# MoE decoder layer: a norm half moved to GpSimd, one expert in 2 MB loads, a list spread over a stage

## The chip, the cores and the metric

The kernel runs on one core of one Trainium2 chip. The metric is the device time of one execution in microseconds (us), the median of several. TensorE (PE) multiplies, VectorE (DVE), ScalarE (ACT) and GpSimd (POOL) work on tiles of 128 partitions, and SyncE (SP) issues the loads from HBM.

## What is computed

A decoder trunk of one layer for 256 tokens of 1024 features in float32: a Mamba-2 mixer, cross-attention into a memory of 256 rows, and a mixture of 32 experts of which each token takes four; then a final norm. Almost all bytes are expert weights: per expert gate_up is 1024 x 2048 and down 1024 x 1024 in float32, 12.58 MB together, 402.7 MB for 32.

```python
    h = h + moe_ffn(rms_norm(h, ffn_norm[i]), w_router, b_router, w_gate_up, b_gate_up, w_down, b_down)
    return rms_norm(h, final_norm)

    # moe_ffn
    logits = (ht @ w_router).astype(jnp.float32) + b_router.astype(jnp.float32)
    top_logits, top_idx = lax.top_k(logits, TOP_K)
    gates = jax.nn.softmax(top_logits, axis=-1)
    ...
        gu = xb @ w_gate_up[e] + b_gate_up[e]
        gate = jnp.minimum(gu[..., :D_FF], SWIGLU_LIMIT)
        up = jnp.clip(gu[..., D_FF:], -SWIGLU_LIMIT, SWIGLU_LIMIT)
        act = (up + 1.0) * (gate * jax.nn.sigmoid(gate * SWIGLU_ALPHA))
        return act @ w_down[e] + b_down[e]
```

## The kernel before

The program is written per engine: each engine has its own list of instructions, ordered by hand, and semaphores tie them together. Mixer and attention take about the first 320 us. What follows is the token norm and the routing, and then the experts.

**Norm and routing.** VectorE adds the attention's output to `h` in four parts (L1800, semaphore `h_ok`). ScalarE squares `h` and takes the root of the mean (semaphore `std`). VectorE then makes `xn`, the normed tokens times the gains `g_ffn`, for tokens 0 to 127 (`norm_chunk(3, 0, ...)`, L1488). The gains are applied in an order in which source and gain are read at a stride of four elements. It computes the router's logits, the largest eight (L1818), the mask of the chosen experts (L1826), then `xn` for tokens 128 to 255 (`norm_apply(3, 1, ...)`, L1488 again, semaphore `normed`). TensorE counts meanwhile from the mask which place each token has with its expert (L933 to L935), between filler matmuls (L914). VectorE makes rank (L1831) and the one-hot matrix of the first two experts (L1834, semaphore `hot_ok`). TensorE's first gather (L946) waits for `hot_ok` and for `normed`. SP waits for `normed` too, before it loads the last two rows of expert 1's gate_up over `h` and `g_ffn`.

**Experts.** Each expert has 64 slots for each of up to four chunks of its tokens; the first 64 tokens are handled in the regular stage, and what overflows would be worked off after the experts from a list (with these inputs TensorE also has to know whether there is one). A stage `regular(i, c)` is expert `2i + c`. On TensorE it is: transposes of the scatter rows (L968), gate_up as 64 matmul instructions in four quarters (L985, semaphore `gu_used` after each), for odd experts half of the gather for the next pair (L960), the down product of the expert before in two halves (L1013, semaphore `dn_used`), transposes of this expert's gate_up for VectorE (L1000), the scatter of the expert before into four banks of sums (L1023), and for odd experts the other half of the gather. VectorE reads out gate_up (L1863), adds biases (L1871) and does SwiGLU up to L1882. Even and odd experts' gate_up weights have a buffer each (`ring`, `odd_ring`, 8 MB), and down has one of 4 MB (`ring`).

**Loads.** SP issues the weights in order. Expert 3 and 31 come in four pieces of 2 MB, each when `gu_used` says that this quarter of the buffer is read (`reload_pieces`, L376); other experts in two groups of 4 MB, each when two quarters are read (`reload_gate_up`, L390). Down comes in two halves of 2 MB (L379). From expert 5 on SP runs a loop over pairs.

**Middle.** Between experts 16 and 17 TensorE leaves its loop and runs `biases_and_list`: it transposes the gates (L1081), which ScalarE copies into `scatT`, multiplies them with the down biases into the sums (L1087), counts tokens (L1091), and goes forward and back with VectorE to make the list of overflowing chunks (L1094 to L1098). All engines then read the number of its entries.

## Time and profile before

| | us |
|---|---|
| median of 3 runs | 1248.57 |
| the runs | 1247.25, 1248.57, 1249.79 |
| the profiled execution | 1247.7 |
| its span in the trace | 1245.9 |
| TensorE busy | 1175.0 (94%) |
| VectorE busy | 391.1 (31%) |
| ScalarE busy | 275.9 (22%) |
| GpSimd busy | 7.5 (1%) |
| DMA, mean over the span | 365 GB/s, 454.30 MB |

The span is what the trace covers; the execution's own time is 1.8 us longer. All times in rows are counted from the span's start. Mean rates tell little here, since the first third loads little. A row of windows gives for a stretch: its length, busy time and instruction count of PE, of its weight loads (PEld), of DVE, ACT and POOL, then TensorE's granted clock as a share of 2.4 GHz, the mean busy share of the 16 DMA engines, and GB/s. A row of the chain gives start, length and what the end of the program was waiting for at that time. A row of a timeline gives start, length, engine, line, operation, output and input with shapes, and in brackets how long the engine had been idle and who ended that. An SP row's time is that of the issue, and its length covers several issues where it says x2. A row of groups gives line, engine, operation, shapes and count, then busy time in us and the mean of one in ns.

### The profile page before, as it was taken

The page shows a single profiled execution, that of the slowest core. Times are in us where ns is not written, and L with a number is a line of the kernel's source. Part 1 is how long each engine was busy: PE and PEld are TensorE (multiplying, and loading weights), DVE is VectorE, ACT ScalarE, POOL GpSimd, SP SyncE. Part 2 cuts the span into 40 slices and gives each one's busy share as a digit, 9 for nine tenths or more (in the row PEclk, how much of TensorE's full clock was granted, in tenths as well). Part 3 has the DMA queues.
Part 4 walks back from the last instruction along what each step waited for, and adds up shares of the span by engine and source line. Part 5 has one row for each costly group of instructions (what it writes and reads, how often), then busy time and mean ns, then how long its engine had stood idle before and what let it go on. Part 6 is the DMA issues. An engine that isn't in the chain of part 4 may idle for free.

```text
span 1245.9 us, 15217 instructions
## 1 busy us (share of the span) xinstructions
PE 1175.0 (94%) x6198; PEld 621.5 (50%) x6198; DVE 391.1 (31%) x703; ACT 275.9 (22%) x421; POOL 7.5 (1%) x27
## 2 busy tenths in 40 slices
PE   9999999999999999998988999899999998999996
PEld 8998887898634433333333333334433333343432
DVE  5987677546312211111111112102211111112112
ACT  5655566345211101011000011001101011011102
POOL 1000000000000000000000000000000000000000
PEclk9999999999999999999999999989999999999999
DMA  9454333469799999999999999999999999999996
GB/s 340 155 203 142 129 135 136 162 262 378 304 407 413 434 426 429 431 431 430 433 433 430 429 436 426 433 417 430 436 426 430 429 431 430 432 423 428 432 424 249
DMA packets 49191, 454.30 MB, mean 365 GB/s; under 512 B 5692, under 2 KB 5860, under 8 KB 30084
## 3 DMA queue, kind: packets, MB, share of 16 engines
q1 hardware_dynamic: 48976, 453.73, 87.7%
q8 instruction: 26, 0.43, 0.1%
q10 hardware_dynamic: 180, 0.07, 0.0%
q14 instruction: 9, 0.07, 0.0%
HBM read 452.74 MB, written 1.05 MB: 364 GB/s over the span
## 4 chain that ended last, share of the span: by engine, by line
PE 53%; DMA 42%; DVE 3%; issue 1%; DVEq 1%; SPq 1%; ACT 0%
DMA ring<-in_moe_w_down 41%; PE ps L985 14%; PE ps L1013 11%; PE ps L647 3%; PE ps L649 3%; PE ps L648 3%; PE ps L1023 2%; PE ps L960 2%; PE ps L662 1%; PE ps L664 1%; PE ps L663 1%; PE ps L779 1%; DMA wring<-in_ssd_w_in 1%; DVE wlo L1504 1%; PE ps L1000 1%
## 5 line engine op out<-in xcount | busy, mean ns | idle before, releaser
L1013 PE MATMUL ps<-ring,wring 128*64 128x512 f32 x960 | 216.5, 597 | 49.3 <-DMA ring<-in_moe_w_down 49.3
L985 PE MATMUL ps<-odd_ring,wring 128*64 128x512 f32 x1024 | 225.5, 598 | 0.9 <-DVE wring L1871 0.8
L985 PE MATMUL ps<-ring,wring 128*64 128x512 f32 x1024 | 223.5, 594 | 0.0
L1136 ACT ACTIVATE wring<-ps 128x512 f32<-128x512 f32 (+2 forms) x101 | 52.4, 535 | 499.8 <-PE ps L985 424.4
L1013 PEld LDWEIGHTS ps<-ring,wring 128*64 128x64 f32 x960 | 65.1, 137 | 188.7 <-issue 112.5
L1863 DVE COPY wring<-ps 128x512 f32<-128x512 f32 x32 | 22.1, 691 | 404.7 <-PE ps L985 404.7
L985 PEld LDWEIGHTS ps<-odd_ring,wring 128*64 128x64 f32 x1024 | 73.7, 138 | 141.6 <-issue 139.6
L985 PEld LDWEIGHTS ps<-ring,wring 128*64 128x64 f32 x1024 | 71.9, 137 | 139.3 <-issue 139.1
L1871 DVE TENSOR_TENSOR wring<-ps,bguT 128x512 f32<-128x512 f32 x64 | 41.2, 685 | 296.7 <-PE ps L1000 296.7
L1136 ACT ACTIVATE ysb<-ps 128x512 f32<-128x512 f32 x36 | 21.4, 596 | 260.6 <-PE ps L1013 246.4
L960 PEld LDWEIGHTS ps<-wring 128*128 128x128 f32 x480 | 55.8, 191 | 23.5 <-issue 23.5
L1023 PE MATMUL ps<-ysb,wring 64*128 64x512 f32 x256 | 63.6, 615 | 0.7 <-ACT ysb L1136 0.7
L960 PE MATMUL ps<-wring 128*128 128x128 f32 x480 | 61.5, 281 | 0.0
L1504 DVE TENSOR_TENSOR wlo<-wring,lo_ring 128x2048 fp32r<-128x2048 f32 x23 | 52.2, 2286 | 11.3 <-ACT lo_ring L1136 11.3
L1136 ACT ACTIVATE lo_ring<-wring 128x2048 fp32r<-128x2048 f32 x24 | 45.4, 1930 | 10.1 <-PE ps L649 5.6
L664 PE MATMUL ps<-hi_ring,wlo 128*128 128x256 f32 x160 | 45.3, 283 | 0.0
L1000 PEld LDWEIGHTS ps<-cst,wring 128*128 128x128 f32 x256 | 27.4, 141 | 26.9 <-issue 25.2
L648 PE MATMUL ps<-wlo,hi_ring 128*128 128x512 f32 x96 | 37.4, 389 | 0.0
L1000 PE MATMUL ps<-cst,wring 128*128 128x128 f32 x256 | 35.0, 280 | 0.9 <-DVE wring L1863 0.9
L1136 ACT ACTIVATE wring<-wring 128x512 f32<-128x512 f32 x32 | 20.2, 630 | 60.7 <-DVE wring L1875 60.7
L1023 PEld LDWEIGHTS ps<-ysb,wring 64*128 64x128 f32 x256 | 22.0, 186 | 22.5 <-issue 20.9
L1538 DVE SCALAR_TENSOR_TENSOR ring<-ps,parT,ring 128x255 f32<-128x255 f32 (+2 forms) x72 | 31.1, 476 | 1.8
(312 smaller groups left out, 1311.6 us busy)
## 6 DMA issues: line engine op xcount, KB each, us to landing
ring<-in_moe_w_down SPq DMA_DIRECT2D x59, 2048.0 KB, 25.3
ring<-in_moe_w_gate_up SPq DMA_DIRECT2D x28, 4096.0 KB, 22.9
odd_ring<-in_moe_w_gate_up SPq DMA_DIRECT2D x26, 4096.0 KB, 24.7
wring<-in_ssd_w_in SPq DMA_DIRECT2D x9, 2048.0 KB, 8.5
odd_ring<-in_moe_w_gate_up SPq DMA_DIRECT2D x9, 2048.0 KB, 15.7
ring<-in_moe_w_down SPq DMA_DIRECT2D x10, 1024.0 KB, 33.8
wring<-in_xa_w_kv SPq DMA_DIRECT2D x4, 2048.0 KB, 8.0
wring<-in_ssd_w_out SPq DMA_DIRECT2D x4, 2048.0 KB, 7.9
```

The source lines that it names most:

```text
L647: mm(ps[bank][:, :], xh[:, k0 + k, tok], wh, start=start and k == 0, stop=False)
L648: mm(ps[bank][:, :], xh[:, k0 + k, tok], wl, start=False, stop=False)
L649: last = mm(ps[bank][:, :], xl[:, k0 + k, tok], wh, start=False, stop=stop and k == KD - 1)
L664: last = mm(dst, wl[:, c0:c0 + P], x_hl[0][:, k, :], start=False, stop=k == KD - 1)
L960: last = mm(ps[G_BANK][:, P * m:P * (m + 1)], xn[:, t, P * k:P * (k + 1)], onehot[:, t, :, :], start=t == 0, stop=t == TC - 1)
L985: last = mm(ps[a][SLOTS * half:SLOTS * (half + 1), :], xs[:, m, c % 2, :], w[:, kk, c0:c0 + 512], start=s + kk == 0, stop=s + kk == GP)
L1000: last = tr(ps[a][:, P * j:P * (j + 1)], gus[:, c0:c0 + P], ident)
L1013: last = mm(ps[D_BANK][SLOTS * half:SLOTS * (half + 1), :], act[:, k, :], w[:, kk, 512 * half:512 * (half + 1)], start=k == 0, stop=k == K ...
L1023: last = mm(ps[4 + 2 * t + half][:, :], rows[r, P * t:P * (t + 1)], ysb[r, :], start=False, stop=True, skip_group_check=True)
L1136: return nc.scalar.activation(out_, in_, func, **kw)
L1504: v.tensor_tensor(lo_, raw_, hi.bitcast(F32), ALU.subtract).then_inc(wl_ok, 1)
L1871: v.tensor_tensor(gu[:, a, :, :, :], ps[a][:, :].rearrange("p (j h s) -> p j h s", j=4, h=2), b4[:, a, :, :].unsqueeze(3).to_broadcast([P, ...
```

## The change

- GpSimd gets two instructions behind its last one: the product of `h` and `g_ffn` for tokens 128 to 255, once `std` says that the root is done, and the product with the reciprocal root, once VectorE has made that (new semaphore `rst_ok`). The second raises `normed`. VectorE's L1488 for these tokens goes.
- Expert 4's gate_up comes in four pieces of 2 MB like expert 3's.
- SP's loop goes; its issues are written out per expert, in the same order. The counts of the semaphores `g_ready` are computed by a new `transfers`.
- TensorE's pairs 0 and 1 are written out, the loop runs over pairs 2 to 7, pair 8 is written out, and a second loop runs over 9 to 14.
- `biases_and_list` is split into four parts, which run inside the stage of expert 18 instead of between 16 and 17. The gates' transposes go to another PSUM bank (3 instead of 2) and are copied by ScalarE to a place of their own, `gateT`. VectorE's part is split in two, ahead of SwiGLU and behind it.

VectorE's rows at the norm, before (L1824 takes the chosen logits out, L1826 makes the mask, L1831 rank, L1834 the one-hot):

```order
L1824 MATCH_REPLACE rank<-mx,lg 128x32 x2
L1826 TENSOR_TENSOR mask<-rank,lg 128x64
L1488 SCALAR_TENSOR_TENSOR wring<-hs,rst 128x1024
L1831 SCALAR_TENSOR_TENSOR rank<-ps,mask 128x2x32
L1834 TENSOR_TENSOR wring<-iota,rank 128x256
```

And now (lines are 36 to 38 higher in the changed kernel):

```order
L1862 MATCH_REPLACE rank<-mx,lg 128x32 x2
L1864 TENSOR_TENSOR mask<-rank,lg 128x64
L1867 SCALAR_TENSOR_TENSOR rank<-ps,mask 128x2x32
L1870 TENSOR_TENSOR wring<-iota,rank 128x256
L1875 TENSOR_TENSOR gate<-gate,mask 128x64
```

The norm of the second token half left VectorE's list. It stands at the end of GpSimd's, behind the products of the mixer (`lo_ring`) that were GpSimd's last work:

```order
L561 CAST iota<-iota_i 128x128
L562 CAST col<-col_i 128x3
L566 TENSOR_TENSOR lo_ring<-by,rank 128x1024 x2
L571 TENSOR_TENSOR wring<-hs 128x1024
L576 TENSOR_SCALAR wring<-wring,rst 128x1024
```

The last two rows are new. SP's rows from expert 3's pieces on, before (`odd_ring` 128x4096 is a 2 MB piece, 128x8192 a 4 MB group):

```order
L376 DMA odd_ring<-in_moe_w_gate_up 128x4096 x4
L379 DMA ring<-in_moe_w_down 128x4096 x2
L390 DMA ring<-in_moe_w_gate_up 128x8192 x2
L379 DMA ring<-in_moe_w_down 128x4096 x2
L492 UNCONDITIONAL_BRANCH
```

And now:

```order
L381 DMA odd_ring<-in_moe_w_gate_up 128x4096 x4
L384 DMA ring<-in_moe_w_down 128x4096 x2
L381 DMA ring<-in_moe_w_gate_up 128x4096 x4
L384 DMA ring<-in_moe_w_down 128x4096 x2
L395 DMA odd_ring<-in_moe_w_gate_up 128x8192 x2
```

The third row, expert 4, is four pieces now, and no loop follows. TensorE's rows at the list, before, from the end of expert 16's stage (L1013 down, L1000 transposes, L1023 scatter) to expert 17's gate_up:

```order
L1013 MATMUL ps<-ring,wring 64x512 x16
...
L1000 MATMUL ps<-cst,wring 128x128 x8
L1023 MATMUL ps<-ysb,wring 128x512 x4
...
L1081 MATMUL ps<-cst,gate 32x128 x2
L1087 MATMUL ps<-wring 128x512 x4
L1091 MATMUL ps<-cst,mask 128x1 x2
L1094 MATMUL ps<-cnt,cst 128x1
L1096 MATMUL ps<-pick,col 1x16
...
L968 MATMUL ps<-cst,wring 128x128 x2
...
L985 MATMUL ps<-odd_ring,wring 64x512 x32
```

And now, inside expert 18's stage (L999 gate_up, L1027 down, L1014 transposes, L1037 scatter):

```order
L1082 MATMUL ps<-cst,gate 32x128 x2
L999 MATMUL ps<-ring,wring 64x512 x32
L1091 MATMUL ps<-wring,wdt 128x512 x4
L1095 MATMUL ps<-cst,mask 128x1 x2
L1027 MATMUL ps<-ring,wring 64x512 x16
L1101 MATMUL ps<-cnt,cst 128x1
L1014 MATMUL ps<-cst,wring 128x128 x8
L1037 MATMUL ps<-ysb,wring 128x512 x4
L1106 MATMUL ps<-pick,col 1x16
L1107 MATMUL ps<-pick,col 1x16
L1108 MATMUL ps<-cst,cnt 1x1
L1148 TENSOR_LOAD lst_i
```

The same products stand between the stage's own parts; the reading of the count (L1148) still follows the last of them. The diff, cut to its core:

```diff
@@ -59,6 +59,9 @@
 GS = GR // 2
 RSLOTS = 8
 MIDDLE = 8
+
+BY_PIECES = (3, 4, 31)
+AHEAD = ((0, 4), (25, 2), (26, 0))
 HSLOTS = 4
 WARM = 17
 
...
+        gateT = part(wdt_f, 0, SEQ)
...
-        def g_loads(n, c):
-
-
-            extra = (0 if n == GP + 1 else 1) if n >= GP else 0 if c < 2 else 1 if n else 2
-            if n % GS == 0:
-                return c // 2 + 1 + extra
-            return min(c // 2, 1) + 1 + extra + (1 if n >= GP and c >= NE - 1 else 0)
+        def transfers(n, e):
+
+
+            if e % 2 != n // GP:
+                return 0
+            if e == 1:
+                return 1 if n == GP + 1 else 2
+            if e == 2:
+                return 2 if n else 3
+            return 1 if e == 0 or e in BY_PIECES or n % GS == 0 else 0
+
+        def g_loads(n, e):
+            return sum(transfers(n, x) for x in range(e + 1))
...
-            def reload_pieces(e):
-
-                for s in range(GP):
+            def reload_pieces(e, pieces_):
+
+                for s in pieces_:
                     sp.wait_ge(gu_used, GP * (e - 2) + s + 1)
                     load_gate_up(sp, e, e % 2, s)
...
-            reload_pieces(3)
-            reload_down(1, 0, 1)
-            reload_gate_up(4, 0, 4)
-            reload_down(2, 0, 2)
-            with sp.Fori(1, PAIRS - 4, 1) as i:
-                for c in (1, 2):
-                    reload_gate_up(2 * i + (c + 2), i, c + 2)
-                    reload_down(2 * i + c, i, c)
-            reload_gate_up(NE - 5, 0, NE - 5, range(0, GJ // 2))
-            reload_down(NE - 7, 0, NE - 7)
-            reload_gate_up(NE - 5, 0, NE - 5, range(GJ // 2, GJ))
-            for e in range(NE - 6, NE - 3):
-                reload_down(e, 0, e)
-                reload_gate_up(e + 2, 0, e + 2)
-            reload_down(NE - 3, 0, NE - 3)
-            reload_pieces(NE - 1)
+            for c in range(1, NE - 2):
+                e = c + 2
+                ahead = [n for first, n in AHEAD if c >= first][-1]
+                for part_, s0, s1 in ((0, 0, ahead), (1, ahead, GP)):
+                    if part_:
+                        reload_down(c, 0, c)
+                    if e in BY_PIECES:
+                        reload_pieces(e, range(s0, s1))
+                    else:
+                        reload_gate_up(e, 0, e, range(s0 // GS, s1 // GS))
...
+            pool.wait_ge(ld_g, 16)
+            pool.wait_ge(std, 2 * 3 + TC)
+            nc.gpsimd.tensor_tensor(xn[:, 1, :].rearrange("q (k p) -> q k p", k=GR),
+                                    h[:, 1, :].rearrange("q (p k) -> q k p", k=GR),
+                                    g_ffn.rearrange("q (p k) -> q k p", k=GR), ALU.mult)
+            pool.drain()
+            pool.wait_ge(rst_ok, 1)
+            nc.gpsimd.tensor_scalar(xn[:, 1, :], xn[:, 1, :], rst[:, 3, 1:2], None, ALU.mult).then_inc(normed, 1)
...
-                    pe.wait_ge(g_ready[n], 16 * i + 16 * g_loads(n, c) if n % GS == 0 else 16 * g_loads(n, expert))
+                    pe.wait_ge(g_ready[n], 16 * i + 16 * (g_loads(n, expert) - (expert - c) // 2) if n % GS == 0 else
+                               16 * g_loads(n, expert))
...
-            def regular(i, c, expert, gathers=True):
-
-                scatter_transpose(i, c)
-                pe.wait_ge(gate_b, 2 * i + c)
-                pe.wait_ge(up_b, 2 * i + c)
-                gate_up(i, c, expert)
-                if gathers:
-                    gather_half(i, 1, 0)
-                down(i, c - 1)
-                transposes(i, c)
-                scatter(i, c - 1)
-                if gathers:
-                    gather_half(i, 1, 1)
-
-            def biases_and_list():
+            def turn_gate():
 
                 pe.wait_ge(gate_ok, 1)
+                pe.wait_ge(xsb_ok, MIDDLE + 2)
                 for t in range(TC):
-                    last = tr(ps[D_BANK][0:NE, P * t:P * (t + 1)], gate[:, t, :], ident)
+                    last = tr(ps[G_BANK][0:NE, P * t:P * (t + 1)], gate[:, t, :], ident)
                 last.then_inc(gT_ps, 1)
+
+            def biases_and_counts():
+
                 pe.wait_ge(gT_ok, 1)
                 pe.wait_ge(ld_bdn, 16)
                 for n in range(2):
                     for t in range(TC):
-                        mm(ps[4 + 2 * t + n][:, :], scatT[0:NE, P * t:P * (t + 1)],
+                        mm(ps[4 + 2 * t + n][:, :], gateT[0:NE, P * t:P * (t + 1)],
                            bdn[0:NE, 512 * n:512 * (n + 1)], start=False, stop=True, skip_group_check=True)
                 pe.wait_ge(mask4_ok, 1)
                 for t in range(TC):
-                    last = mm(ps[D_BANK][:, 256:257], mask4[:, t, :], ones[:, 0:1], start=t == 0, stop=t == TC - 1)
+                    last = mm(ps[G_BANK][:, 256:257], mask4[:, t, :], ones[:, 0:1], start=t == 0, stop=t == TC - 1)
                 last.then_inc(cnt_ps, 1)
+
+            def places():
+
                 pe.wait_ge(val_ok, 1)
-                mm(ps[D_BANK][:, 258:259], stri, cnt[:, 0:1], start=True, stop=True).then_inc(pos_ps, 1)
+                mm(ps[G_BANK][:, 258:259], stri, cnt[:, 0:1], start=True, stop=True).then_inc(pos_ps, 1)
+
+            def overflow_list():
+
                 pe.wait_ge(pick_ok, 1)
-                mm(ps[D_BANK][0:1, 272:288], col[:, 0:1], pick[:, :], start=True, stop=True)
-                mm(ps[D_BANK][0:1, 288:304], col[:, 1:2], pick[:, :], start=True, stop=True)
-                mm(ps[D_BANK][0:1, 304:305], cnt[:, 0:1], ones[:, 0:1], start=True, stop=True).then_inc(lst_ps, 1)
-                pe.wait_ge(lst_ok, 1)
+                mm(ps[G_BANK][0:1, 272:288], col[:, 0:1], pick[:, :], start=True, stop=True)
+                mm(ps[G_BANK][0:1, 288:304], col[:, 1:2], pick[:, :], start=True, stop=True)
+                mm(ps[G_BANK][0:1, 304:305], cnt[:, 0:1], ones[:, 0:1], start=True, stop=True).then_inc(lst_ps, 1)
+
+            def regular(i, c, expert, gathers=True, lists=False):
+
+                scatter_transpose(i, c)
+                if lists:
+                    turn_gate()
+                pe.wait_ge(gate_b, 2 * i + c)
+                pe.wait_ge(up_b, 2 * i + c)
+                gate_up(i, c, expert)
+                if lists:
+                    biases_and_counts()
+                if gathers:
+                    gather_half(i, 1, 0)
+                down(i, c - 1)
+                if lists:
+                    places()
+                transposes(i, c)
+                scatter(i, c - 1)
+                if lists:
+                    overflow_list()
+                if gathers:
+                    gather_half(i, 1, 1)
 
             pe.wait_ge(hot_ok, 1)
...
-            regular(0, 1, 1)
-            regular(0, 2, 2, False)
-            with pe.Fori(1, MIDDLE, 1) as i:
-                regular(i, 1, 3)
-                regular(i, 2, 4, False)
-            biases_and_list()
+
+            for i in range(0, 2):
+                regular(i, 1, 2 * i + 1)
+                regular(i, 2, 2 * i + 2, False)
+            with pe.Fori(2, MIDDLE, 1) as i:
+                regular(i, 1, 5)
+                regular(i, 2, 6, False)
+            regular(MIDDLE, 1, 2 * MIDDLE + 1)
+            regular(MIDDLE, 2, 2 * MIDDLE + 2, False, True)
+            pe.wait_ge(lst_ok, 1)
             extra = pe.value_load(lst_i[0:1, 32:33], min_val=0, max_val=MAX_EXTRA)
-            with pe.Fori(MIDDLE, PAIRS - 1, 1) as i:
-                regular(i, 1, 3)
-                regular(i, 2, 4, False)
+            with pe.Fori(MIDDLE + 1, 15, 1) as i:
+                regular(i, 1, 2 * MIDDLE + 3)
+                regular(i, 2, 2 * MIDDLE + 4, False)
             last_experts(PAIRS - 1)
...
-            def regular(i, c, gathers=True):
+            def regular(i, c, gathers=True, lists=False):
 
                 scatter_out(i, c)
+                if lists:
+                    act_.wait_ge(gT_ps, 1)
+                    fn(gateT[0:NE, :], ps[3][0:NE, 0:SEQ], ACT.Copy).then_inc(gT_ok, 1)
...
-            act_.wait_ge(gT_ps, 1)
-            fn(scatT[0:NE, :], ps[2][0:NE, 0:SEQ], ACT.Copy).then_inc(gT_ok, 1)
+            regular(MIDDLE, 1)
+            regular(MIDDLE, 2, False, True)
             act_.wait_ge(lst_ok, 1)
             extra = act_.value_load(lst_i[0:1, 32:33], min_val=0, max_val=MAX_EXTRA)
-            with act_.Fori(MIDDLE, PAIRS - 1, 1) as i:
+            with act_.Fori(MIDDLE + 1, PAIRS - 1, 1) as i:
...
-            v.reciprocal(rst[:, 3, 1:2], nrm[:, 3, 1:2])
+            v.reciprocal(rst[:, 3, 1:2], nrm[:, 3, 1:2]).then_inc(rst_ok, 1)
...
-            norm_apply(3, 1, xn, h, g_ffn)
-            dve.drain()
...
-            def regular(i, c, gathers=True, out=act):
+            def regular(i, c, gathers=True, out=act, lists=False):
...
+                if lists:
+                    overflow_places()
                 swiglu(i, c, 2 * i + c, out)
-
-            def overflow_list():
+                if lists:
+                    overflow_list()
+
+            def overflow_places():
...
+            def overflow_list():
+
...
-            overflow_list()
+            regular(MIDDLE, 1)
+            regular(MIDDLE, 2, False, lists=True)
```

## Rows read from the trace of the kernel before

**Rows 1.** Windows: stretch, length, engines' busy times, clock, DMA share, GB/s.

```profile
324.00:348.00 24.00, 22.42 (x112) 12.47 (x114) 7.09 (x27) 3.37 (x6) 0.00 (x0) 0.93 0.84 315
384.00:400.00 16.00, 16.00 (x78) 5.38 (x76) 0.69 (x1) 0.60 (x1) 0.00 (x0) 1.00 0.97 400
460.00:800.00 340.00, 307.21 (x1514) 118.81 (x1510) 55.50 (x120) 31.40 (x57) 0.00 (x0) 1.00 1.00 431
800.00:835.00 35.00, 31.14 (x134) 12.58 (x135) 6.44 (x19) 2.58 (x5) 0.00 (x0) 0.85 1.00 421
```

**Rows 2.** The chain that ended last: start, us, what.

```profile
817.49 15.92 PE ps L985 x64
...
1073.11 13.88 PE ps L985 x64
...
1093.86 1.02 PE ps L1000 x8
...
1097.16 13.88 PE ps L985 x64
...
1125.19 13.88 PE ps L985 x64
```

**Rows 3.** SP's timeline: issues of weight loads.

```profile
328.90 0.80 SPq L383 DMA_DIRECT2D odd_ring<-in_moe_w_gate_up  x2
335.39 1.19 SPq L460 DMA_DIRECT2D ring<-in_moe_w_gate_up  x2
...
387.56 7.19 SPq L390 DMA_DIRECT2D ring<-in_moe_w_gate_up  x2
...
826.77 7.16 SPq L390 DMA_DIRECT2D odd_ring<-in_moe_w_gate_up  x2
```

**Rows 4.** The chain at the middle, between experts 16 and 17.

```profile
804.54 1.03 PE ps L1000 x8
...
808.27 4.21 PE ps L1087 x8
812.48 0.96 PE ps L1091 x4
...
815.72 1.09 issue
```

**Rows 5.** VectorE's timeline at the norm, and the end of expert 16's SwiGLU.

```profile
322.74 2.13 DVE L1488 SCALAR_TENSOR_TENSOR wring<-hs,rst 128x1024 f32<-128x1024 f32 x1
...
326.69 0.22 DVE L1826 TENSOR_TENSOR mask<-rank,lg 128x64 f32<-128x64 f32 x1
326.83 2.05 DVE L1488 SCALAR_TENSOR_TENSOR wring<-hs,rst 128x1024 f32<-128x1024 f32 x1
...
329.28 0.43 DVE L1834 TENSOR_TENSOR wring<-iota,rank 128x256 f32<-128x256 f32 x1
...
808.28 0.69 DVE L1882 TENSOR_TENSOR wring<-wring 128x512 f32<-128x512 f32 x1
```

**Rows 6.** TensorE's timeline from the rank counts to the first gather.

```profile
327.43 0.39 PE L935 MATMUL ps<-mask,cst 128*128 128x32 f32 x2
...
329.80 4.43 PE L946 MATMUL ps<-wring 128*128 128x128 f32 x23 [1.04 <-DVE wring L1834]
```

**Rows 7.** Groups by line: busy us, mean ns of one.

```profile
L1504 DVE TENSOR_TENSOR wlo<-wring,lo_ring 128x2048 fp32r<-128x2048 f32 x23 | 52.2, 2286 | 11.3 <-ACT lo_ring L1136 11.3
L1488 DVE SCALAR_TENSOR_TENSOR wring<-hs,rst 128x1024 f32<-128x1024 f32 x2 | 4.2, 2090 | 0.1
L561 POOL TENSOR_TENSOR lo_ring<-by,rank 128x1024 fp32r<-128x1024 f32 x2 | 3.8, 1898 | 116.8 <-PE ps L649 116.8
L1485 DVE TENSOR_SCALAR ring<-hs,rst 128x1024 f32<-128x1024 f32 x2 | 1.5, 754 | 0.2
```

**Rows 8.** ScalarE's timeline: the root for tokens 128 to 255.

```profile
322.74 0.29 ACT L1136 ACTIVATE nrm<-nrm 128x1 f32<-128x1 f32 x1
```

**Rows 9.** Timeline of GpSimd and VectorE in the mixer.

```profile
122.28 3.75 POOL L561 TENSOR_TENSOR lo_ring<-by,rank 128x1024 fp32r<-128x1024 f32 x2 [116.81 <-PE ps L649]
...
125.00 3.18 DVE L1504 TENSOR_TENSOR wlo<-wring,uth 128x2048 fp32r<-128x2048 f32 x1
```

11 lines of the change are left out of this document (6 added, 5 removed).

## The prediction

> **What bounds the kernel now.** I read the bandwidth of stretches first, then the chain, then SP's timeline, and the busy shares last: TensorE is busy 94% and the DMA engines are full as well, so shares decide nothing. From 460 to 800 us the stream runs at 431 GB/s with a DMA share of 1.00 [rows 1]; that is its ceiling in this trace. One expert's weights are 12.58 MB, at 431 GB/s 29.2 us. TensorE alone needs less: where it waits for nothing, gate_up groups of the same parity start at 1073.11 and 1125.19 [rows 2], so two experts take 52.08 us and one 26.04. It has 3.2 us to spare per expert.
>
> So from about 340 to 1230 us the kernel is a stream of bytes. **A microsecond counts only if it lets the stream run earlier or closes a stretch below 431.** Such a stretch loses its length times (1 - rate/431): 324 to 348 us loses 6.5, 384 to 400 loses 1.15, 800 to 835 loses 0.81 [rows 1]. The change touches all three. That the chain names PE from 1068 on does not contradict this: TensorE sets the times of the issues there, and the queue is still filled.
>
> **Expert 4 in 2 MB pieces.** SP issues its first group at 387.56 [rows 3], because 4 MB wait for two quarters of expert 2's gate_up. The stream runs down meanwhile; that is the 1.15 us. A gate_up takes 13.88 [rows 2], a quarter of it 3.47, so the first 2 MB can be issued at 384.1, 3.5 us earlier, three times the sag. The second piece is issued at 387.56 as before and needed 4.9 us (2.1 MB at 431 GB/s) behind the first. Later groups are issued as before; TensorE frees 12.58 MB in 26.0 us, which the stream needs 29.2 for, so the margin only grows. **Gain 1.15 us**, bounds 0 (something else than the late issue makes the sag) and 1.3 (its edges too). The two more issues on SP cost nothing: SP waits for TensorE between them.
>
> **List and biases inside expert 18's stage.** In a plain stage gate_up starts 3.30 us behind the transposes (1093.86 to 1097.16 [rows 2]). At the middle the transposes start at 804.54, and gate_up not at 807.84 but at 817.49: bias products 4.21, counts 0.96, rounds with VectorE up to 815.72, and 1.09 of reading the count [rows 2, 4]. That is 9.7 us; and this gate_up takes 15.92 instead of 13.88 [rows 2], in a stretch whose mean granted clock is 0.85 [rows 1]. Sum 11.7 us. The issue that hangs on it came at 826.77 [rows 3], so some 11.7 late, and the stream lost only 0.81. So 10.9 us of delay are free here and only what exceeds them costs.
> Now, in expert 18's stage: 0.8 to turn the gates (transposes and copy, up to 808.27 from the 807.5 at which scatter is done), 4.2 and 1.0, together 6.0 us ahead of the down product, of which 3.2 are spare: 2.8 late. Behind it: the places product, 0.6, a quarter of the 2.3 us between 813.44 and 815.72 [rows 4]; then VectorE ends SwiGLU 4.4 us behind the transposes' start (804.54 to 808.97 [rows 4, 5]), the list takes 0.5 more, reading it 1.09, the scatter rows' transposes 0.3: 6.3 against 3.3 in a plain stage, 3.0 late. Sum 6.4; with 2.0 for a fall of the clock 8.4, below 10.9. TensorE catches up 3.2 per expert, by expert 21. What is queued behind its wait for the list is expert 19's gate_up, and for that waits SP's group for expert 21; both are in the 8.4. VectorE waits for the counts ahead of SwiGLU, whose transposes come behind the down product anyway. **Gain 0.8 us**, bounds 0 and 0.85; over 11.7 it would turn into a loss, 1 us for 1 us.
>
> **The queue written out, loops cut differently.** SP's loop and register steps go, TensorE leaves out a turn of its loop: covered by the waits of both in these stages. Zero, bounds -0.2 and 0.2, estimates from the 3.2 of spare time that would have to fail first.
>
> **The token norm's second half on GpSimd.** This is the uncertain term, because it moves the start of the experts, on which everything up to 384 us hangs. Before, L1488 for tokens 128 to 255 runs on VectorE for 2.05 us from 326.83, behind mask (326.69), and rank and one-hot follow until 329.71; the first gather starts 329.80, 1.04 behind the last filler matmul [rows 5, 6]. Without L1488 the rank counts decide: TensorE ends them at 327.82 (327.43 + 0.39 [rows 6]), then rank 0.3 and one-hot 0.5 make 328.6, or 328.4 with no pauses. A gain of 1.2 to 1.4 us, if GpSimd is done by then.
> GpSimd does it in two steps: a product of h and g_ffn, 128x1024, both read at a stride of four elements, and the product with the scalar. Its only product in this trace, 128x1024 with plain or repeated operands, took 1.90 us [rows 7]. What the stride does shows on VectorE: L1504 takes 2.29 for 2048 contiguous elements, so 1.14 for 1024, and L1488 takes 2.09 for 1024 [rows 7], a factor of 1.8. So the product takes between 1.9 and 3.4; I take the middle, 2.65. The scalar step lies between 0.75 (VectorE's L1485) and 1.9 (GpSimd's product); I take the middle, 1.3 [rows 7]. The root it needs is ready at 323.03 [rows 8].
> It may not start there. GpSimd's second product ended at 126.03; L1504 on VectorE, begun 125.00, took 3.18 instead of 2.29 [rows 7, 9]. So an instruction of VectorE with two operands in SBUF and a GpSimd product did not run at once; the later one waited. Now L1488 for tokens 0 to 127 holds VectorE from 322.74 for 2.13 us [rows 5], so the product runs 324.9 to 327.55. Mask has two SBUF operands, is due 326.69 and waits until 327.55; the rank counts end 328.65. The scalar step runs 327.65 to 328.95, rank beside it (one operand in PSUM), the one-hot, two SBUF operands, 329.0 to 329.5. First gather at 329.6 instead of 329.8: **gain 0.2 us**. Bounds: a gain of 1.4 (nothing collides), and with 3.4 and 1.9 for the two steps the one-hot ends 330.75, a loss of 1.1. I take the value between, since the collision has a row and its absence has none.
> The Trainium skill, SBUF — State Buffer, section "Who interferes with whom", calls this an exclusive lock on a port pair that the two engines share, and the trace agrees for L1504 (3.18 against 2.29). The Trainium skill, GPSIMD Engine Reference, section "Performance pitfalls for Q7 kernels", has reads at a stride over 8 bytes cost half again as much: an estimate of 2.85 us for the product by it, with which the forecast would be 0.2 us later; no run here shows it yet.
> SP too waits for this norm before the last two rows of expert 1, issued 328.90 [rows 3]. Those 2 MB take 4.9 us, and the next issue at 335.39 [rows 3] waits for TensorE; what they win by being earlier is lost there unless TensorE is earlier. So only the first gather's time counts.
>
> **Sum.** 1.15 + 0.8 + 0 + 0.2 = 2.1 us. The profiled execution took 1247.7 us (span 1245.9): 1245.6. The median of three is 1248.57, 0.87 above it; carried over, 1248.57 - 2.1 = **1246.5 us**, 0.17% less, under the 0.2% (2.5 us) that a measurement of this kernel can tell from no change.
>
> **Rivals.**
> (a) GpSimd is hidden whole, first gather at 328.4. For it: its wait is met at 323.03, 5.4 us ahead. Against: L1504's 3.18. Total 1.15 + 0.8 + 1.4 = 3.35, 1245.2; if the pause of 1.04 goes and with it the fall of the clock (mean 0.93 over 24 us [rows 1], that is 3.4 us at half clock, 1.7 lost), 1243.5.
> (b) The collision is worse: the small one-source instruction ahead of mask (L1820) waits for the product as well. Then match_replace and mask are due only at about 328.3, the scalar step is running, and mask starts 329.0; rank counts 1.1, rank and one-hot 0.8, gather 330.9, 1.1 late. Total 1.15 + 0.8 - 1.1 = 0.85: 1247.7. No row shows such an instruction beside GpSimd. The Trainium skill, SBUF — State Buffer, section "Who interferes with whom", says that a tensor_scalar in a 2-port mode takes the pair as well.
> (c) The sags move instead of closing: with SP's issues tied to TensorE, what the stream gains is lost at a later issue point. Total 0.2: 1248.4. Against: TensorE is faster than the stream everywhere behind.
> (d) Slower: GpSimd's product on strided operands is far dearer. Each microsecond over 2.65 delays the first gather by one; at 4.75 all gains are spent, and from 7.25, nearly four times the row's 1.90, the loss can be told. At 8 us: 1246.5 + 5.35 = 1251.8. Against: the factor of 1.8 on VectorE.
>
> **Chances.** Forecast 0.35, (a) 0.25, (b) 0.20, (c) 0.12, (d) 0.08. Under 1246.07 it is faster by over 0.2%: nearly all of (a), and 0.15 of the rest, as the forecast lies 0.4 us from that line while three runs spread over 2.5: 0.40. Slower: (d) and 0.01 of spread, 0.09. Within: 0.51. Range: low 1243.8 (the clock case less some of its 1.7), high 1249.3 ((c) and 0.9 of spread); (d) is left out.
>
> **What would show it.** Windows of the changed kernel: 384 to 400 at 430 GB/s, else the pieces did nothing; around experts 19 to 21 at 430, else the list came too late, and SP's issue for expert 21 says by how much. GpSimd's two rows give their start and length; a product that starts beside L1488 and takes under 3 us refutes the collision, a mask that starts late confirms it, late steps ahead of it confirm (b). The first gather, against the last addition to h, gives the norm term. If both sags are closed and the stream ends less than 1 us earlier though the gather is not late, the view of the kernel as a stream is wrong.

## The result, and the profile after

The changed kernel took **1250.38 us** (median of 20 runs, 1249.44 to 1251.22). The kernel before, run beside it, took 1246.43 (20 runs, 1244.95 to 1249.79); the ratio is **1.0031, interval 1.0024 to 1.0037**, 3.95 us slower. The forecast was 0.17% faster, with a chance of 0.09 for "slower by over 0.2%". It was wrong in sign. The profiled execution took 1249.45 (span 1247.7), 1.75 more than the one before, which with 1247.7 was one of the later ones of its kernel. The 20 times of the kernel before fall mostly into two groups, near 1245.5 and near 1247.4; what may part them comes below.

Windows after (length, engines' busy times, granted clock, DMA share, GB/s), and behind them the window of before at 1090 us:

```profile
324.00:348.00 24.00, 20.23 (x104) 11.72 (x105) 8.22 (x26) 3.27 (x6) 7.51 (x2) 0.93 0.74 274
384.00:400.00 16.00, 16.00 (x76) 5.32 (x74) 0.69 (x1) 0.60 (x1) 0.00 (x0) 1.00 1.00 427
800.00:835.00 35.00, 31.02 (x152) 11.81 (x150) 5.29 (x13) 2.81 (x5) 0.00 (x0) 1.00 1.01 431
1090.00:1100.00 10.00, 10.00 (x52) 3.86 (x50) 2.88 (x7) 1.63 (x4) 0.00 (x0) 1.00 0.85 333
```

```profile
1090.00:1100.00 10.00, 10.00 (x50) 3.81 (x48) 4.60 (x12) 1.61 (x3) 0.00 (x0) 1.00 0.97 390
```

Against [rows 1]: both slow stretches did close, 400 to 427 GB/s and 421 to 431. The start got worse (315 to 274), and a stretch at 1090 us, which the prediction does not mention, fell from 390 to 333.

The start, on GpSimd, VectorE and TensorE of the changed kernel (timelines: start, us, operation):

```profile
323.08 5.58 POOL L571 TENSOR_TENSOR wring<-hs 128x1024 f32<-128x1024 f32 x1 [197.11 <-ACT nrm L1171]
328.84 2.85 POOL L576 TENSOR_SCALAR wring<-wring,rst 128x1024 f32<-128x1024 f32 x1 [0.18 <-issue]
```

```profile
322.64 2.12 DVE L1526 SCALAR_TENSOR_TENSOR wring<-hs,rst 128x1024 f32<-128x1024 f32 x1
...
325.82 2.86 DVE L1858 TENSOR_SCALAR gsum<-mx 128x2 f32<-128x2 f32 x1
...
329.27 0.76 DVE L1864 TENSOR_TENSOR mask<-rank,lg 128x64 f32<-128x64 f32 x1
...
331.27 0.42 DVE L1870 TENSOR_TENSOR wring<-iota,rank 128x256 f32<-128x256 f32 x1
```

```profile
330.08 0.41 PE L946 MATMUL ps<-mask,cst 128*128 128x32 f32 x2 [3.77 <-DVE mask L1864]
...
331.84 4.48 PE L959 MATMUL ps<-wring 128*128 128x128 f32 x24
336.25 4.08 PE L999 MATMUL ps<-ring,wring 128*64 128x512 f32 x18
```

GpSimd's product holds VectorE's L1858, an instruction of two elements per partition that takes 0.17 us otherwise (the same instruction at 325.93 in before), for 2.86 us, until the product ends. Mask, 326.69 before [rows 5], starts at 329.27. The first gather starts at 331.84 instead of 329.80 [rows 6], gate_up at 336.25 instead of 334.27. The Trainium skill, SBUF — State Buffer, section "Who interferes with whom", has a tensor_scalar wait too; the 2.86 agrees. Beside GpSimd's second instruction the wait was short: mask, with two operands in SBUF, began inside it (328.84 to 331.69) and took 0.76 us instead of 0.22, and the one-hot at 331.27 took its usual 0.42. The norm (331.69) and the one-hot (331.69) end together, so either alone would have held the gather as long. SP's issue that waits for the norm comes at 331.72 instead of 328.90.

The issues on SP (timeline):

```profile
337.37 1.19 SPq L471 DMA_DIRECT2D ring<-in_moe_w_gate_up  x2
...
386.10 10.63 SPq L381 DMA_DIRECT2D ring<-in_moe_w_gate_up  x4
...
880.36 7.20 SPq L395 DMA_DIRECT2D odd_ring<-in_moe_w_gate_up  x2
```

Expert 4's first 2 MB go out at 386.10, 1.46 ahead of the group before [rows 3] although everything is 2 us late: 3.4 us were won, as forecast. The middle of the changed kernel, TensorE in expert 18's stage:

```profile
855.60 3.69 PE L1091 MATMUL ps<-wring,wdt 32*128 32x512 f32 x8
859.22 0.60 PE L1095 MATMUL ps<-cst,mask 128*128 128x1 f32 x4
859.76 7.09 PE L1027 MATMUL ps<-ring,wring 128*64 128x512 f32 x32
...
867.02 1.07 PE L1014 MATMUL ps<-cst,wring 128*128 128x128 f32 x8
...
872.87 0.43 PE L981 MATMUL ps<-cst,wring 128*128 128x128 f32 x2 [2.64 <-issue]
873.23 3.23 PE L999 MATMUL ps<-odd_ring,wring 128*64 128x512 f32 x14
```

Gate_up starts 6.2 us behind the transposes of the stage before (867.02 to 873.23) instead of 3.3, so 2.9 late (forecast 3.0); no sag follows.

### The profile page after: what moved, and what is told of

Same layout as the page of the kernel before. It is cut to its first block, busy times and chain, and to the rows that moved or that the text cites. A ratio compares the mean times of both kernels' runs of the same rounds, so it can differ in the third digit from the quotient of the medians.

```text
span 1247.7 us, 14882 instructions
## 1 busy us (share of the span) xinstructions
PE 1173.3 (94%) x6198; PEld 621.4 (50%) x6198; DVE 392.5 (31%) x702; ACT 276.3 (22%) x421; POOL 15.9 (1%) x29
## 3 DMA queue, kind: packets, MB, share of 16 engines
HBM read 452.74 MB, written 1.05 MB: 364 GB/s over the span
## 4 chain that ended last, share of the span: by engine, by line
PE 56%; DMA 41%; DVE 1%; issue 1%; SPq 0%; ACT 0%; DVEq 0%; POOL 0%; POOLq 0%
DMA ring<-in_moe_w_down 41%; PE ps L999 13%; PE ps L1027 11%; PE ps L660 3%; PE ps L662 3%; PE ps L661 3%; PE ps L675 2%; PE ps L676 2%; PE ps L677 2%; PE ps L973 2%; PE ps L1037 2%; PE ps L647 1%; PE ps L792 1%; PE ps L1014 1%; PE ps L771 1%; PE ps L770 1%
## 5 line engine op out<-in xcount | busy, mean ns | idle before, releaser
L1027 PE MATMUL ps<-ring,wring 128*64 128x512 f32 x960 | 218.0, 600 | 51.2 <-DMA ring<-in_moe_w_down 51.2
L999 PE MATMUL ps<-odd_ring,wring 128*64 128x512 f32 x1024 | 223.3, 594 | 0.8 <-DVE wring L1907 0.8
L999 PE MATMUL ps<-ring,wring 128*64 128x512 f32 x1024 | 223.5, 594 | 0.0
L1027 PEld LDWEIGHTS ps<-ring,wring 128*64 128x64 f32 x960 | 65.5, 137 | 191.3 <-issue 114.2
L1171 ACT ACTIVATE wring<-ps 128x512 f32<-128x512 f32 (+1 forms) x100 | 52.1, 537 | 490.7 <-PE ps L999 422.3
L999 PEld LDWEIGHTS ps<-odd_ring,wring 128*64 128x64 f32 x1024 | 73.2, 137 | 139.5 <-issue 137.8
L999 PEld LDWEIGHTS ps<-ring,wring 128*64 128x64 f32 x1024 | 72.0, 137 | 139.3 <-issue 139.1
L1037 PE MATMUL ps<-ysb,wring 64*128 64x512 f32 x256 | 63.6, 615 | 0.7 <-ACT ysb L1171 0.7
L1014 PEld LDWEIGHTS ps<-cst,wring 128*128 128x128 f32 x256 | 27.5, 141 | 26.1 <-issue 24.3
L1014 PE MATMUL ps<-cst,wring 128*128 128x128 f32 x256 | 34.9, 279 | 0.9 <-DVE wring L1899 0.9
L1037 PEld LDWEIGHTS ps<-ysb,wring 64*128 64x128 f32 x256 | 22.0, 186 | 22.5 <-issue 20.9
```

Of the source, the lines that this page charges most:

```text
L999: last = mm(ps[a][SLOTS * half:SLOTS * (half + 1), :], xs[:, m, c % 2, :], w[:, kk, c0:c0 + 512], start=s + kk == 0, stop=s + kk == GP)
L1014: last = tr(ps[a][:, P * j:P * (j + 1)], gus[:, c0:c0 + P], ident)
L1027: last = mm(ps[D_BANK][SLOTS * half:SLOTS * (half + 1), :], act[:, k, :], w[:, kk, 512 * half:512 * (half + 1)], start=k == 0, stop=k == K ...
L1037: last = mm(ps[4 + 2 * t + half][:, :], rows[r, P * t:P * (t + 1)], ysb[r, :], start=False, stop=True, skip_group_check=True)
L1171: return nc.scalar.activation(out_, in_, func, **kw)
```

## The experiments

All ratios stand against the kernel before, run on the same chip, with 95% intervals. The expectations name three theories, A, B and C; C is that the norm's move is the whole loss and the rest of the change is worth nothing in the end.

### Taking the change apart

```diff
 # norm_back: the changed kernel, norm on VectorE again
-            pool.wait_ge(ld_g, 16)  ... (both GpSimd instructions)
+            norm_apply(3, 1, xn, h, g_ffn)
 # norm_only: the kernel before, with that block on GpSimd and nothing else
 # no_pieces: norm_back, with
-BY_PIECES = (3, 4, 31)
+BY_PIECES = (3, 31)
 # queue_only: the kernel before, with SP's queue written out as in the change, expert 4 in groups
 # list_only: the kernel before, with only list and biases inside expert 18's stage (pair 8 written out for it)
```

> The changed kernel with the norm of tokens 128 to 255 back on VectorE; expert 4's pieces, the list in expert 18's stage and the written-out queue stay. Theory A (the pace of the stream is set by the slowest of the 16 DMA engines; the sags at 384 and 826 us were only the faster engines waiting for it, and what else the change costs comes with the written-out code): first gather back at 329.8, and about 1.8 us slower than before (ratio 1.0014). Theory B (the stream's mean rate counts, each closed sag gives its loss): about 2 us faster than before (0.9984). Rival C (the norm costs all of the 3.9): same as before.

> The kernel before with nothing but the norm of tokens 128 to 255 moved to GpSimd. All theories: GpSimd's product again about 5.6 us, the small tensor_scalar of VectorE near 2.9 us, the first gather 2.1 us later. Theories A and B: 2.1 us slower than before (1.0017). Rival C: 3.9 us slower (1.0031).

> As e1_norm_back, and expert 4 in 4 MB groups again; list in the stage and written-out queue stay. Theory A: the same as e1_norm_back within 0.3 us; the sag at 384 to 400 is back in the mean rate, but the slowest DMA engine ends expert 4's groups no later. Theory B: 1.1 us slower than e1_norm_back.

> The kernel before with only SP's queue written out per expert, same order and sizes. Theory A: between 0 and 1 us slower, since the additional instruction fetches go through the DMA engines and each holds one of them for about 0.6 us. Theory B: 0, and a tie would also say that the remaining cost lies with TensorE's written-out pairs or the list.

> The kernel before with only the overflow list and biases inside expert 18's stage. Theory C (a stretch in which the stream runs under 431 GB/s is the faster DMA engines waiting for the slowest, and closing it gives nothing): the stretch 814 to 843 us runs at 430 GB/s instead of 418, and the ratio is 1.0000, within 0.0006. Rival (bytes count one for one): 0.8 us faster, 0.9993.

> The changed kernel itself, beside the others on the same chip. Its ratio should be 1.0031 again; it is what the two kernels with more or fewer steps are compared with. If the parts add, it equals the norm's part (1.0036) plus what the rest is worth (1.0005 by the kernel without the norm's part, 0.9998 by the queue alone), that is 1.0030 to 1.0041.

```
kernel                    median   ratio   interval
norm on VectorE again     1245.70  1.0005  0.9996 to 1.0014
norm's move alone         1248.95  1.0036  1.0022 to 1.0050
norm again, no pieces     1246.38  1.0006  0.9997 to 1.0016
SP's queue alone          1245.92  0.9998  0.9989 to 1.0007
list and biases alone     1245.50  0.9997  0.9988 to 1.0006
the changed kernel again  1250.10  1.0031  1.0021 to 1.0041
```

The norm's move carries the whole loss. Everything else together is 1.0005: a gain of 1.95 us (0.9984, theory B) is outside its interval, a loss of 1.0014 (A) at its edge. The norm's move alone excludes the 1.0017 of A and B. C is the one that holds. In that run's profile the first gather came at 332.94, 3.1 us late instead of the expected 2.1, but it ran faster, and gate_up started at 336.27 as in the changed kernel. With the list alone the stretch did close:

```profile
814.00:843.00 29.00, 25.71 (x136) 11.40 (x134) 4.73 (x9) 3.67 (x7) 0.00 (x0) 1.00 1.01 432
```

It ran at 418 GB/s before, and 432 brought 0.4 us with an interval of -0.7 to +1.5; the 0.8 of the forecast is not excluded by this run alone, and the pieces alone (1.0005 against 1.0006) are not told apart either. Only their sum is.

That comparison says little about a closed sag, for there was none to close. From 384 to 400 us, first without the pieces and then in pool_cost (the kernel before, but for three idle-time instructions on GpSimd, see below):

```profile
384.00:400.00 16.00, 16.00 (x79) 5.46 (x76) 0.69 (x1) 1.05 (x2) 0.00 (x0) 1.00 1.03 427
384.00:400.00 16.00, 16.00 (x78) 5.49 (x75) 0.69 (x1) 0.96 (x2) 0.00 (x0) 1.00 1.02 423
```

The expectation that the sag would be back was wrong. It is deepest in before (400) and in SP's queue alone (406), the two profiles of VectorE's norm in its old place in which TensorE's clock fell at the gather, so that gate_up started at 334.2. There the 4 MB group was issued at 387.5, here, with gate_up at 332.5 and 332.6, at 385.8 and 385.9.

### What the move on GpSimd costs

```diff
 # pool_cost: the kernel before, three extra instructions on GpSimd while VectorE is idle
+            pool.wait_ge(gu_part, 1)
+            nc.gpsimd.tensor_tensor(bdn..."q (k p) -> q k p", xn[:, 1, :]..., xn[:, 0, :]..., ALU.mult)
+            pool.drain()
+            nc.gpsimd.tensor_scalar(bdn, bdn, rst[:, 3, 1:2], None, ALU.mult)
+            pool.drain()
+            nc.gpsimd.tensor_tensor(bdn, xn[:, 1, :], xn[:, 0, :], ALU.mult)
```

> The kernel before with three more instructions on GpSimd while VectorE has nothing with two operands in SBUF to do (behind the first group of gate_up): a product of 128x1024 with the strides that the changed kernel's has, a product with a scalar, and a product of 128x1024 with plain operands; their result is overwritten by the down biases. If the 5.58 us of the changed kernel's product hold a wait for VectorE's L1526 (until 324.76, 1.7 us), the strided one takes 3.8 to 3.9 here; if they hold none, 5.6. Scalar step: 1.9 to 2.1 if the mask's 0.5 was in the 2.85, else 2.85. Plain product: 1.9 as in the trace of before.

```profile
333.78 4.04 POOL L567 TENSOR_TENSOR wring<-wring 128x1024 f32<-128x1024 f32 x1 [207.78 <-PE ps L995]
338.00 2.85 POOL L571 TENSOR_SCALAR wring<-wring,rst 128x1024 f32<-128x1024 f32 x1 [0.18 <-issue]
341.00 2.36 POOL L573 TENSOR_TENSOR wring<-wring 128x1024 f32<-128x1024 f32 x1
```

With nothing beside it the strided product takes 4.04 us, the plain one 2.36 (expected 1.9), the scalar step 2.85. So the 5.58 hold 1.5 to 1.7 of waiting for L1526 (which ends at 324.76), and the scalar step's 2.85 holds no wait. The stride costs a factor of 1.7. The Trainium skill, GPSIMD Engine Reference, section "Performance pitfalls for Q7 kernels", has half again as much; measured against the plain product here it is 1.7.

### Is it GpSimd, or only the late gate_up?

```diff
 # norm_first: the kernel before, nothing on GpSimd, VectorE's norm (and half of it twice) ahead of mask
+            norm_half(0)
+            dve.drain()
+            norm_apply(3, 1, xn, h, g_ffn)
             v.tensor_tensor(mask[:, :, :], rest, lg[:, :, :], ALU.not_equal).then_inc(mask_ok, 1)
-            norm_apply(3, 1, xn, h, g_ffn)
 # fillers, fillers_8: the changed kernel, TensorE kept busy in the wait for mask
-            keep_warm(1, 3)
+            keep_warm(1, 16)     (fillers)
+            keep_warm(1, 8)      (fillers_8)
```

> The kernel before with nothing on GpSimd, but with VectorE's scaling of tokens 128 to 255 (2.05 us) ahead of the mask instead of behind it, and ahead of that a scaling of half its columns (1.13 us) which is done again by it and serves only to take time. The mask is then ready at about 330.0 and the first gather at 331.8, as in the changed kernel, with the same 3.8 us in which TensorE is idle. Theory C (only the time at which gate_up can begin counts, whoever causes it): gate_up starts at 336.2, ratio 1.0031 (1.0022 to 1.0036). Rival G (GpSimd's instructions do harm beyond the late mask, by their traffic or at the end of the norm): at most 1.0020.

> The changed kernel, with 13 more filler matmuls on TensorE in the 3.8 us in which it waits for the mask ahead of the rank counts. GpSimd and VectorE do what they do in the changed kernel, so the first gather stays at 331.8. Theory K (a part of the loss is TensorE's clock, which falls to half behind this longer gap): the granted clock does not fall at 331 us, the first gathers take 2.9 us for 24 instead of 4.5, gate_up starts at 334.7 instead of 336.25, and the kernel is 1.3 to 1.6 us faster than the changed kernel on the same chip, ratio 1.0020 against the kernel before. Theory L (the lateness of the gather alone): no difference to the changed kernel, ratio 1.0031. Rival: the fall only comes later, as it does in other profiles (505, 854 us), with the same result as L.

> The changed kernel with 5 more filler matmuls in the 3.8 us in which TensorE waits for the mask, where the run with 13 more had made TensorE itself 1.5 us late (gather at 333.4, yet gate_up at 336.23 as the gathers ran at full clock). Some 2.1 us are filled and 1.7 stay open, more than the 1.04 behind which the clock falls in some executions of the kernel before. Theory K (time = gate_up's start; clock falls behind an idle stretch of TensorE, but not always behind a short one): where it does not fall, gather at 331.85, gate_up at 334.7, span 1.5 us shorter than the changed kernel's, ratio 1.0019; where it falls as before, 336.25 and 1.0031. So a ratio between 1.0019 and 1.0031, and in the profiled execution gate_up's start and the granted clock at 331 say which. Theory L (lateness of the gather alone): 1.0031 in either case.

Measured: norm_first 1250.90, ratio 1.0040 (1.0026 to 1.0054); fillers 1249.31, 1.0020 (1.0010 to 1.0030); fillers_8 1249.10, 1.0025 (1.0016 to 1.0034). TensorE's timeline in norm_first, then in fillers, then in fillers_8:

```profile
330.00 0.64 PE L933 MATMUL ps<-mask,cst 128*128 128x32 f32 x2 [3.68 <-DVE mask L1838]
...
333.15 4.27 PE L946 MATMUL ps<-wring 128*128 128x128 f32 x24
337.35 3.23 PE L985 MATMUL ps<-ring,wring 128*64 128x512 f32 x14
```

```profile
333.38 2.92 PE L959 MATMUL ps<-wring 128*128 128x128 f32 x24
336.23 4.08 PE L999 MATMUL ps<-ring,wring 128*64 128x512 f32 x18
```

```profile
330.15 0.41 PE L946 MATMUL ps<-mask,cst 128*128 128x32 f32 x2 [1.62 <-DVE mask L1864]
...
331.95 4.35 PE L959 MATMUL ps<-wring 128*128 128x128 f32 x24
336.23 4.08 PE L999 MATMUL ps<-ring,wring 128*64 128x512 f32 x18
```

Norm_first loses as much as the changed kernel without touching GpSimd, so a late mask is enough for the loss and rival G's limit of 1.0020 is excluded. It is not the same wait to the end: the clock fell at 329.3, inside TensorE's idle time, so that the gather started at 333.15 and gate_up at 337.35, 1.1 later than expected. A harm of GpSimd's own of up to about 1 us would not show beside that. Norm_first also parts the two things that are late in the changed kernel: here SP's issue behind the norm came at 329.84, 1.9 earlier than there, and it did not help; gate_up did count. In fillers the gather starts 1.5 us later still, since the fillers themselves run until 331.8, but it runs at 2.4 GHz throughout (2.92 us for 24 instead of 4.48) and gate_up starts at the same 336.23. The expectation that the gather would stay at 331.8 was a miscount of the fillers. In fillers_8 the clock fell in spite of the 5 more fillers, and gate_up starts at 336.23 again. So theory K's best case, gate_up at 334.7, was not met by either, and whether these two win anything against the changed kernel (1.0020 and 1.0025 against 1.0031) is open: the intervals overlap. Theory L is wrong in that gate_up, not the gather, marks the time: fillers has the latest gather of all and is not slower.

### An earlier gather

```diff
 # norm_split: the kernel before, norm in two halves of 128x512
             v.tensor_tensor(mask[:, :, :], rest, lg[:, :, :], ALU.not_equal).then_inc(mask_ok, 1)
-            norm_apply(3, 1, xn, h, g_ffn)
+            norm_half(0).then_inc(half_ok, 1)
...          (behind the one-hot)
+            norm_half(1).then_inc(normed, 1)
 # TensorE: wait for half_ok ahead of first_gather(0, ...), for normed ahead of first_gather(1, ...)
 # split_all: the same in the changed kernel (early pieces, list in stage 18, queue written out)
```

> The kernel before, with VectorE's scaling of tokens 128 to 255 cut into two instructions of 128x512 (the columns of the gathers' first half, then of the second); the second stands behind the one-hot, and TensorE waits for it ahead of the second group of gathers. Nothing goes to GpSimd. Theory C (what the changed kernel lost is the lateness of the first gather, 1 us for 1 us or a little more): the half instruction takes 1.0 to 1.1 us and ends before the rank counts (327.8), the one-hot ends about 1.0 earlier, the first gather starts at about 328.8 instead of 329.8, and the kernel is 0.9 to 1.0 us faster, ratio 0.9992. Rival (a start of the experts that is earlier is lost again at the later sags, as the early pieces were): the gather is 1.0 earlier and the ratio is 1.0000. Rival (the clock): with a gap of only 0.1 us ahead of the gather TensorE's clock does not fall at 330 us, and the gain is 1.0 + 1.4 = 2.4 us, ratio 0.998.

> The changed kernel with the norm on VectorE again, in two halves of 128x512 as above: early pieces, list inside expert 18's stage, queue written out, and the earlier first gather. Theory C: first gather at 328.8 and what the halves give alone, 0.9 to 1.0 us, beside 0 for the rest: ratio 0.9992 (0.9985 to 1.0000). Rival (the closed sags let an earlier start through, which the open ones would swallow): faster than the halves alone by 0.5 to 1.0 us, ratio 0.9985. Rival (skew of the DMA engines takes all of it): 1.0005 as without the halves.

> The changed kernel with the norm split on VectorE, once more: ratio 0.9989 again, 0.9980 to 0.9998, if the gain is real; 1.0000 if it was chance. By gate_up's start (331.7 against 332.7 to 334.3) it should be 1.0 us faster or more.

Norm_split: 1245.04, ratio 0.9992 (0.9982 to 1.0001). Split_all: 1245.03, 0.9989 (0.9979 to 0.9998), and when run again 1245.39, 0.9994 (0.9985 to 1.0003). VectorE and TensorE in norm_split:

```profile
326.79 1.13 DVE L1488 SCALAR_TENSOR_TENSOR wring<-hs,rst 128x512 f32<-128x512 f32 x1
328.01 0.23 DVE L1842 SCALAR_TENSOR_TENSOR rank<-ps,mask 128x64 f32<-128x64 f32 x1
328.31 0.43 DVE L1845 TENSOR_TENSOR wring<-iota,rank 128x256 f32<-128x256 f32 x1
328.65 1.14 DVE L1488 SCALAR_TENSOR_TENSOR wring<-hs,rst 128x512 f32<-128x512 f32 x1
```

```profile
328.84 2.92 PE L947 MATMUL ps<-wring 128*128 128x128 f32 x24
331.69 5.37 PE L986 MATMUL ps<-ring,wring 128*64 128x512 f32 x24
```

The gather came at 328.84, as expected, and the gain is 1.0 us by the medians, with 1.0000 just inside the interval. The two of split_all say 1.4 and 0.7. These have the lowest ratios of all kernels here, with and without the rest of the change; the intervals of two of the three reach 1.0000, and all overlap those of the list alone and the queue alone.

**One line through all.** Start of gate_up and time of the profiled execution:

```
kernel            gate_up  clock fell at the gather  time
norm_split        331.69   no                        1243.85
split_all         331.67   no                        1245.35
split_all again   331.84   no                        1245.44
no_pieces         332.52   no                        1245.83
pool_cost         332.61   no                        1245.37
norm_back         332.68   no                        1245.21
list_only         333.02   no                        1246.18
queue_only        334.19   yes                       1246.55
before            334.27   yes                       1247.70
fillers           336.23   no                        1249.19
fillers_8         336.23   yes                       1249.43
after             336.25   yes                       1249.45
changed again     336.27   yes                       1247.91
norm_only         336.27   yes                       1248.72
norm_first        337.35   yes                       1250.83
```

A straight line through the 15 has a slope of 0.96 us per us and misses them by 0.5 on the average, 1.2 at most. That is the test of "stream of bytes" for the first 330 us: a microsecond there counts in full. It is one execution of each kernel, and where the norm is on GpSimd, SP's issue is late too.

The table also shows the second part of the loss. Behind TensorE's idle 1.03 to 1.05 us the clock went to 1.2 GHz in 3 of 9 profiles (the unrolled kernels below included), behind 1.6 to 3.8 us in 5 of 5, behind at most 0.55 in none of 4. The length of the idle time does not decide it alone: elsewhere in the kernel before TensorE was idle for 1.64 us, and the clock stayed at 2.4 GHz from 460 to 800 us [rows 1]:

```profile
562.28 3.22 PE L1013 MATMUL ps<-ring,wring 128*64 128x512 f32 x14 [1.64 <-DMA ring<-in_moe_w_down]
```

A fall makes the 24 gathers 1.6 us longer (4.54 against 2.92). Kernels with VectorE's norm in its old place so have gate_up at 332.5 to 333.0 without a fall and at 334.2 with one; I take it that the two groups of times of the kernel before are this, but its other executions have no trace. The changed kernel has it at 336.25 and 336.27 in its two profiles. On the average of the nine that is 336.25 - 332.7 - 0.5 = 3.0 us, the lower end of the measured 3.0 to 4.6.

### Why the closed stretches paid nothing

The 16 DMA engines do not finish a transfer together. From the trace I took, for the last row of an expert's down weights, the times at which its 16 completions arrived: first, last, and the distance.

```
expert's        before                  changed
down row   first   last   dist     first   last   dist
 1         388.0   391.8   3.9     390.5   392.2   1.7
 2         418.6   421.1   2.5     419.8   422.4   2.6
 5         506.2   508.7   2.5     507.5   510.6   3.2
16         827.6   830.0   2.4     828.8   832.0   3.2
17         858.0   859.7   1.8     858.0   861.3   3.3
19         916.4   918.2   1.8     916.4   920.6   4.1
25        1082.0  1083.8   1.8    1082.0  1086.1   4.1
26        1102.1  1103.3   1.1    1104.7  1105.6   0.9
29        1189.8  1190.9   1.1    1192.4  1193.3   0.9
```

At expert 25 the fastest engine of the changed kernel has made up its whole delay (1082.0 in both), the slowest is 2.3 us behind and stays so. At 1090 us the distance falls from 4.1 to 0.9, as the first engines run out of work and the last does not: this is the new sag. It is deep (333 GB/s) in this execution; the changed kernel run again has 380 there, norm_back 395. TensorE needs a whole row, so it goes by the last engine: its down product of 591.50 in before starts as the last completion of that row arrives, at 591.5. In "before" the sags at 384, 814 and 1090 us are the same thing: distance 3.9 to 2.5, 2.4 to 1.8, 1.8 to 1.1. An expert takes the last engine 29.2 us in an undisturbed stretch; across the first sag it took 29.3 (391.8 to 421.1) and across the second 29.7 (830.0 to 859.7), while the first engine took 30.6 and 30.4. So in before the two sags cost the last engine 0.1 and 0.5 us, not 1.15 and 0.8, and by this count no more than that could be won. Why is the last one later? The distance grows near the times at which the queue of instruction fetches has a packet (16,384 bytes, 0.9 to 1.5 us on one engine): in the changed kernel from 2.6 to 3.2 with the one at 503 us, from 3.3 to 4.1 with the one at 905. Those at 481 and 881 changed nothing, and no row says which engine served a fetch, so this is a suspicion, not a reading. The pages' queue lines, before and after:

```profile
q8 instruction: 26, 0.43, 0.1%
```

```profile
q8 instruction: 30, 0.49, 0.2%
```

The four more lie at 481, 503, 881 and 905 us, in code that the change writes out. A kernel with more of them tests it:

```diff
 # unroll_7 (unroll_3: range(1, 4), then the loop from 4)
-            with pe.Fori(1, MIDDLE, 1) as i:
+            for i in range(1, MIDDLE):
                 regular(i, 1, 3)
                 regular(i, 2, 4, False)
```

> The kernel before with TensorE's first loop (7 turns of two experts each) written out 7 times; the instructions that it executes stay the same. Theory S (instruction fetches hold up single DMA engines, and the slowest sets the end): about one more fetch of 16 KB per expert, 12 to 14 more between 450 and 800 us, each near 1 us on one of 16 engines; the distance of the last from the first engine at the end of each expert's down weights, 2.5 us in the kernel before, grows with them; the slowest engine carries 1 to 3 of them, so the last landings, and the end, come 0.9 to 2.7 us later, ratio 1.0007 to 1.0022, while the mean (13 us spread over 16) would give only 0.8. Rival N (the fetches are lost in the noise, or the loop's own jumps cost as much): 1.0000, within 0.0005.

> The same with only the first 3 turns written out ahead of a loop of 4: a smaller dose, 6 more fetches. Theory S: distance of the engines up by 0 to 1 us by 650 us, ratio 1.0002 to 1.0013, between the kernel before and the one written out 7 times. Rival N: 1.0000, within 0.0005.

> The kernel with TensorE's first loop written out 7 times, once more, for a second profiled execution. Theory S (instruction fetches between 450 and 800 us cost time behind 450): wherever the execution stands at 340 us, it loses 1.5 to 2.5 us between there and the end, against the kernel before, and the engines' distance grows to 3.6 us or more by 720 us; the ratio is 1.0015 to 1.0029. Rival E (the loss is made in the mixer, by code that moved in memory): late by 1 to 4 us at 320 us again, and by no more at the end.

```
kernel          median   ratio   interval          fetches 330 to 1200 us
unroll_7        1249.64  1.0029  1.0019 to 1.0038  19
unroll_7 again  1250.23  1.0042  1.0027 to 1.0058  19
unroll_3        1248.07  1.0017  1.0008 to 1.0026  13
before                                              7
```

Both doses cost time, with the same instructions executed, and all three ratios lie above what theory S had expected (1.0022 and 1.0029 at most for unroll_7, 1.0013 for unroll_3). A fetch takes 0.9 to 1.5 us in all profiles, not the 0.6 that was assumed for the queue alone. The page of unroll_7:

```profile
q8 instruction: 39, 0.64, 0.2%
```

The down rows in unroll_7 again: the last engine is 1.0 us ahead of the kernel before at expert 5 (507.7), 0.5 behind at 9 (626.1), 1.6 behind at 16 (831.6), 2.3 behind at 29 (1193.2). That is 3.3 us lost behind 450, more than the 1.5 to 2.5 of theory S and far more than the mean (12 fetches of 1 us over 16 engines, 0.8). The distance grew in steps and not with every fetch: here from 2.2 to 3.7 between 567 and 626 us, near the fetches at 587 and 615; in unroll_3 from 3.0 to 4.4 at 622, behind the one at 614; in the first profile of unroll_7 from 2.7 to 3.6 at 597, near the one at 593. The others from 500 to 780 us left it as it was. Unroll_3 lost 1.3 us behind 450 in the same way of counting. That written-out code costs time there is shown by the two doses; that the fetches do it, by holding the last engine, is argued from these coincidences. The megabytes delivered by 827 us came as early as in before, and the loss in them appears between 1060 and 1107 us (from 0.25 ahead to 1.5 behind), as in the changed kernel.

A part of the ratios is made much earlier. At the rank counts (326.96 in before) the three profiles of written-out code stood 3.7 us late (unroll_7), 0.8 (again) and 1.0 (unroll_3), the other kernels with VectorE's norm in its old place at most 0.4; the first of them lost 2.0 more behind 450. So rival E is right in part: the delay is there in all three, made in the first 60 us, and its cause stays open. The line through gate_up's start takes it out. By gate_up (337.81, 333.46 and 333.67) and time (1253.40, 1248.94 and 1248.31) the three lie 2.8, 2.5 and 1.7 us above that line, about 2.6 for 12 more fetches and 1.7 for six; the line itself misses single kernels by up to 1.2.

For the list I compare split_all and norm_split, which start alike. The last engine is at 827.4 and 827.2 at expert 16, at 858.0 and 856.4 at expert 17, at 916.4 and 914.9 at 19, so split_all loses 1.5 us. It loses it by 858.0, ahead of its two additional fetches at 876 and 901, so those did not do it; why the last engine was held there stays open. In the medians the two are alike (1245.03 and 1245.04). More than that is not known of the two.

## Why the prediction was wrong

- **Start, the norm term: failed, and this alone turned the sign.** The forecast took 2.65 and 1.3 us for GpSimd's steps; they take 4.04 and 2.85 alone, and the first one 5.58 in place. Both are outside the ranges set (to 3.4, and to 1.9). The nearest row, a product of 1.90 [rows 7], had other operands; a plain product of two tiles took 2.36, and the scalar step had no row of its kind, so "not above the product" was an unfounded bound. Not the number alone but the step failed: by how much GpSimd's two instructions hold up VectorE and the gather. Forecast was a gather 0.2 us earlier, measured one 2.04 later, and gate_up 2.0 later.
- **The collision: right in kind, wrong in its victim.** It was forecast to stop mask; it stopped the two-element instruction three steps ahead (L1820 of before), as rival (b) says, for 2.86 us. With a product of 2.65 that would have been 1.1 late; it was 2.04. Rival (d), a dearer product, was right too: the product ended at 328.66, 1.1 later than the forecast's 327.55. They were priced apart, each with the other at its forecast value, and their sum, 2.2, is near the 2.04. The chance of a told loss, 0.09, held only (d) at 7.25 us.
- **The clock was priced on one side only.** Rival (a) gives 1.7 us back if the pause goes. That a longer pause can add falls was not in the sum. The fall came in 3 of 9 profiles with the short pause and in all five with the longer one; by these counts it is 1.0 of the 3.95. The traces show the falls, the share is an estimate from few profiles.
- **The two sags: place right, worth wrong.** Issue 3.4 us earlier, list 2.9 late at the second place, no sag behind: all as forecast. But 1.15 + 0.8 counted bytes of all engines, and the end is set by the last one, which lost 0.1 and 0.5. And the 1.15 belonged to the profiled execution: with gate_up at 332.5 the stretch ran at 423 and 427 GB/s without any pieces, by the same sum 0.15 to 0.3 us. The text's own condition, both sags closed, the gather not late, and the stream not 1 us earlier, came true in norm_back (1.0005): the view as a stream holds for the start, and fails for sags in which only the faster engines wait. The stretch at 1090 us, between the groups of [rows 2], has no part in the forecast; rival (c), the sags move instead of closing, had the right worth for this term, and its time of 1248.4 is 1.9 above the forecast. Its mechanism, a loss at a later point, fits the profile of the changed kernel (333 GB/s at 1090 us) and not norm_back's (395).
- **The queue written out: right** (0.9998), for SP. For TensorE "zero" was wrong in kind: written-out code cost time in both doses above. How much of it the changed kernel pays for its four additional fetches is not shown; with everything but the norm's move it ties (1.0005).
- **The base.** 1248.57 was the median of three; 20 runs gave 1246.43. Carrying over the 0.87 above the profiled time was noise. It moved the forecast in us, not in per cent.

## What to carry to other kernels

Before an operation moves to an idle engine, list every instruction of the old engine that runs beside it, the two-element ones first, and price the slowest form of the new one; half of the same instruction on the old engine was worth 1 us here, and the whole of it on the idle one cost 3 to 4. The 1 us is from medians (0.9992), with no change just inside the interval. In a kernel bound by its stream, look at the last of the DMA engines, not at GB/s: the two dips cost 1.15 and 0.8 us by the mean rate and 0.1 and 0.5 by the last engine. Ask of a second profile whether a dip is there at all. Written-out code is not free there: TensorE's loop written out, with 12 more fetches, cost 2 to 3 us behind the start.

## What the runs showed of the hardware

- GpSimd, 128x1024 float32: product at a stride of four 4.04 us, plain 2.36, with a scalar 2.85. VectorE's 128x1024 norm takes 2.05, its half 1.13.
- A VectorE instruction on 128x2 elements waited 2.7 us for a GpSimd product, while those from PSUM and MAX8 ahead of it ran at their usual 0.41 and 0.29. Beside GpSimd's scalar step, a VectorE instruction with two operands in SBUF took 0.76 us instead of 0.22 and did not wait for the step's end.
- Instruction fetches are counted on the same 16 DMA engines as the weights, 16,384 bytes in 0.9 to 1.5 us each. The last of the 16 engines ended a row 1.7 to 4.1 us behind the first in the stream of these two profiles, the distance held over hundreds of us, and it fell to 0.9 to 1.1 where the queue ran low at 1090 us.
- At this gather TensorE's clock fell to 1.2 GHz behind idle stretches of 1.0 us in 3 of 9 profiles, and behind 1.6 us and more in all five. At 560 us it stayed at 2.4 GHz behind 1.64 us.
